# Mixer steps of an eight-head delta rule in another order: preparation in two parts, a denser solve, a later inverse, four heads' norms earlier

## What is computed

```python
# 8 heads of 128, 512 tokens in chunks; the reference uses chunks of 64, the kernel solves blocks of 128
q, k, v = silu(causal_depthwise_conv(qkv, conv_w, width=4)); q, k = l2_normalize(q), l2_normalize(k)
decay = exp(where(causal, gc_i - gc_j, -inf))           # gc: cumulated log decay per head
a_mat = where(strict, beta_i * (k k^T) * decay, 0)
u, w  = triangular_solve(a_mat + I, [beta v, beta exp(gc) k])
qk    = where(causal, (q k^T) * decay, 0)
for chunk: v_new = u - w S; o = q_dec S + qk v_new; S = S * exp(g_last) + k_dec^T v_new
o = rms_norm(o, dn_norm_g) * silu(z)
merged = sigmoid(g_pool) * (pool @ pool_proj) + sigmoid(g_dn) * (o @ dn_proj)
x = x + gate * (merged @ mix_w_out)
```

## Time and profile before

| | us |
|---|---|
| median of 3 runs | 1993.36 (1989.79 to 1993.92) |
| the profiled execution | 1994.52, span 1992.5 |
| TensorE busy | 1908.3 (96%) |
| VectorE busy | 915.5 (46%) |
| ScalarE busy | 810.4 (41%) |
| GpSimd busy | 130.6 (7%) |
| mean granted TensorE clock | 0.979 |

### The profile page before, as it was taken

One profiled execution on the slowest core, in us unless ns is written; L12 is line 12 of the kernel. 1 busy time (PEld: TensorE's weight loads), 2 busy tenths in 40 slices (PEclk: granted clock), 3 DMA queues, 4 the chain that ended last, 5 costly groups with the idle time before them and its releaser, 6 DMA issues.

```text
span 1992.5 us, 22201 instructions
## 1 busy us (share of the span) xinstructions
PE 1908.3 (96%) x8899; PEld 1467.7 (74%) x8899; DVE 915.5 (46%) x1644; ACT 810.4 (41%) x1324; POOL 130.6 (7%) x158
## 2 busy tenths in 40 slices
PE   7999999999989899999999998899899999999997
PEld 4666666666778788888876776777777878888886
DVE  4655566556433433333236765367244443333322
ACT  5555555556632322322224652463363333222221
POOL 0111111110001000000100010001000110000010
PEclk9999999999999999999999998999999999999999
DMA  5434333432232223222314222121212422322331
GB/s 207 159 129 151 136 143 131 150 127 94 85 128 95 76 95 104 95 95 91 102 41 164 85 75 64 38 74 59 64 43 95 140 82 96 96 95 95 95 98 61
DMA packets 56686, 201.95 MB, mean 101 GB/s; under 512 B 6639, under 2 KB 7095, under 8 KB 55945
## 3 DMA queue, kind: packets, MB, share of 16 engines
q1 hardware_dynamic: 44616, 158.32, 23.9%
q0 software_dynamic: 11968, 42.21, 5.9%
HBM read 195.23 MB, written 5.28 MB: 101 GB/s over the span
## 4 chain that ended last, share of the span: by engine, by line
PE 86%; DVE 6%; ACT 5%; DMA 2%; issue 1%; POOL 0%; SPq 0%; DVEq 0%; ACTq 0%; POOLq 0%
PE ps L1010 24%; PE ps L1013 24%; PE ps L1011 24%; PE ps L1061 2%; PE ps L1051 2%; PE ps L1097 2%; PE ps L1085 2%; DVE wL L1285 1%; DVE a L1556 1%; DVE a L1559 1%; PE ps L1073 1%; ACT wH L1630 1%; PE ps L1034 1%; PE ps L1140 1%; PE ps L1133 1%
## 5 line engine op out<-in xcount | busy, mean ns | idle before, releaser
L1010 PE MATMUL ps<-hH,wH 128*128 128x512 f32 (+1 forms) x1640 | 688.7, 420 | 20.0 <-DVE hL L1325 12.3
L1013 PE MATMUL ps<-hH,wL 128*128 128x512 f32 (+1 forms) x1640 | 647.5, 395 | 0.6 <-DVE wL L1285 0.6
L1011 PE MATMUL ps<-hL,wH 128*128 128x512 f32 (+1 forms) x1640 | 646.3, 394 | 0.0
L1285 DVE TENSOR_TENSOR wL<-wr,wH 128x1024 fp32r<-128x1024 f32 (+2 forms) x285 | 343.9, 1207 | 501.2 <-ACT wH L1630 501.1
L1630 ACT ACTIVATE wH<-wr 128x1024 fp32r<-128x1024 f32 (+2 forms) x285 | 295.2, 1036 | 279.7 <-PE ps L1013 267.5
L1010 PEld LDWEIGHTS ps<-hH,wH 128*128 128x128 f32 (+1 forms) x1640 | 312.5, 191 | 128.6 <-issue 61.5
L1011 PEld LDWEIGHTS ps<-hL,wH 128*128 128x128 f32 (+1 forms) x1640 | 312.3, 190 | 73.5 <-issue 14.9
L1013 PEld LDWEIGHTS ps<-hH,wL 128*128 128x128 f32 (+1 forms) x1640 | 311.1, 190 | 70.2 <-DVE wL L1285 2.0
L1013 PE MATMUL ps<-gffn,wL 128*128 128x512 f32 x352 | 137.0, 389 | 0.0
L1010 PE MATMUL ps<-gffn,wH 128*128 128x512 f32 x352 | 137.0, 389 | 0.0
L1011 PE MATMUL ps<-gffn,wH 128*128 128x512 f32 x352 | 136.9, 389 | 0.0
(11 more groups left out here) (286 smaller groups left out, 1958.6 us busy)
## 6 DMA issues: line engine op xcount, KB each, us to landing
wr<-wst SPq DMA_DIRECT2D x268, 512.0 KB, 3.5
a<-wfd POOLq DMA_DIRECT2D x54, 512.0 KB, 4.6
xT<-wfd POOLq DMA_DIRECT2D x18, 512.0 KB, 6.9
wr<-wst SPq DMA_DIRECT2D x16, 384.0 KB, 3.0
xT<-xin SPq DMA_DIRECT2D x8, 256.0 KB, 5.2
xT<-xin SPq DMA_DIRECT2D x2, 1024.0 KB, 6.0
xsave<-xT SPq DMA_DIRECT2D x1, 2048.0 KB, 8.9
a<-wfd POOLq DMA_DIRECT2D x8, 256.0 KB, 3.6
```

What stands on the lines that cost most here:

```text
L1010: e.matmul(o, hi, xh[k], start=k == 0, stop=False)
L1011: e.matmul(o, hi, xl[k], start=False, stop=False)
L1013: i = e.matmul(o, lo, xh[k], start=False, stop=k == t.nk - 1)
L1285: e.tensor_tensor(dst, x, hi.bitcast(F32), ALU.subtract).then_inc(s[name], 1)
```

## The change

- `out0`: `mod` comes after the fourth result tile, not inside the first.
- `conv_act` is due 6 ticks after the eighth k is begun, not 8.
- The sums of q come at Q+39+j (were Q+43+2j) and the norms of q at Q+44 (was Q+50).
- `prep` comes at Q+52+3j, a tick earlier, and only TensorE's three groups, VectorE's mask addition and ScalarE's exponentials stay in it. VectorE's three products and GpSimd's are a new step `prep_end` at Q+56+3j. ScalarE takes the four exponentials of `dt` before the one of the bank. `sol_send` goes to Q+66.
- The 30 `solve` steps take 20 ticks, not 30; `sol_back` is at Q+100 (was Q+110).
- The inverse begins at Q+125 (was Q+120), the recursion at Q+139 (was Q+134); in it one fill tick is added ahead of each `rec_r`.
- In the second half the squares and norms of heads 0 to 3 are put at Q+104 and Q+112, with other buffers (`hb`), and P5 and P6 wait for them. After the recursion heads 4 to 7 follow, the norms 8 ticks later; `zd_out` of heads 0 to 2 comes 2, 4 and 6 ticks after it, that of head 3 after 8, those of 4 to 7 as before.

```diff
             r = sig("xr")
             self.whole(Tile("res0", src("l0_w_out", 128 * c, 16), self.pb01.take()[1], "g", ("xr", r), c=c, xr=r),
-                       then=(lambda: square(c - 1)) if c > 0 else (lambda: add("mod")))
+                       then=(lambda: square(c - 1)) if c > 0 else None)
+            if c == 3:
+                add("mod")
...
                 if k == 7:
-                    at(clock[0] + 8, conv_act, a)
+                    at(clock[0] + 6, conv_act, a)
...
+        def prep_end(h):
+            add("prep_end", **heads[h]["prep"])
...
+        def head_squares(g):
+            add("head_squares", g=g, hq=[sig("hq") for _ in range(4)], oe=4 * g + 4)
...
                 at(at_k + 2 * j, l2_sum, h, kl)
-                at(Q + 43 + 2 * j, l2_sum, h, ql)
-                at(Q + 53 + 3 * j, prep, h)
+                at(Q + 39 + j, l2_sum, h, ql)
+                at(Q + 52 + 3 * j, prep, h)
+                at(Q + 56 + 3 * j, prep_end, h)
                 at(Q + 51 + 8 * j, v_turn, h)
             at(at_k + 7, l2, "k", kl)
-            at(Q + 50, l2, "q", ql)
-            at(Q + 63, lambda: add("sol_send", half=half, pa2=self.count["pa2"]))
+            at(Q + 44, l2, "q", ql)
+            at(Q + 66, lambda: add("sol_send", half=half, pa2=self.count["pa2"]))
             for k in range(1, 31):
-                at(Q + 79 + k, lambda k=k: add("solve", half=half, k=k))
-            at(Q + 110, lambda: add("sol_back", half=half))
+                at(Q + 79 + (2 * k) // 3, lambda k=k: add("solve", half=half, k=k))
+            at(Q + 100, lambda: add("sol_back", half=half))
             for j, step in enumerate(("t", "p5", "y5", "p6", "y6")):
-                at(Q + 120 + 3 * j, inverse, half, step)
+                at(Q + 125 + 3 * j, inverse, half, step)
+            if half == 1:
+                at(Q + 104, head_squares, 0)
+                at(Q + 112, head_norms, 0)
...
-            while clock[0] < Q + 134:
+            while clock[0] < Q + 139:
                 fill(1)
...
                 if t > 0:
+                    fill(1)
                     d["ks"], d["rr"] = sig("ks"), [sig("rr") for _ in range(4)]
...
-        add("head_squares", hq=[sig("hq") for _ in range(DNH)], oe=self.count["oe"])
...
+        head_squares(1)
         B = clock[0]
-        at(B + 6, head_norms, 0)
-        at(B + 13, head_norms, 1)
+        at(B + 8, head_norms, 1)
         for h in range(DNH):
-            at(B + 16 + 3 * h, zd_out, h)
+            at(B + 2 + 2 * h if h < 4 else B + 8 + 3 * h, zd_out, h)
...
+        hb = [P5[:, 0:512], P6[:, 0:512], P6[:, 512:1024], vT[0], tq[4], tq[5], tq[6], tq[7]]
...
                     e.tensor_tensor(v3(dt), v3(ps[b][:]), per4(C("mneg")), ALU.add).then_inc(s["px2"], 1)
+                elif what == "prep_end":
+                    hh = d["h"] % 4
+                    b, b2, b3 = d["banks"]
+                    at, dt = AT[hh], DT[d["dt"]]
                     w.wait_ge(s["pkk"], d["pkk"])
                     w.wait_ge(s["pxs"], d["pxs"])
...
                     w.wait_ge(s["px2"], d["px2"])
-                    e.activation(b[:], b[:], ACT.Exp).then_inc(s["px1"], 1)
                     w.wait_ge(s["bd"], 6)
                     for t in range(4):
                         col = 8 * t + d["h"]
                         i = e.activation(b4(dt, t), b4(dt, t), ACT.Exp, bias=ngc[:, col:col + 1])
                     i.then_inc(s["pxs"], 1)
+                    e.activation(b[:], b[:], ACT.Exp).then_inc(s["px1"], 1)
...
+                    w.wait_ge(s["oe"], d["oe"])
+                    if d["g"] == 0:
+                        w.wait_ge(s["dvt"], DNH)
+                    for h in range(4 * d["g"], 4 * d["g"] + 4):
+                        e.activation(hb[h], oD[h], ACT.Square).then_inc(s["hq"], 1)
...
-                elif what == "prep":
+                elif what == "prep_end":
                     at = AT[d["h"] % 4]
                     w.wait_ge(s["pa1"], d["pa1"])
```

More of the change, by code:

```diff
@@ L603, in inverse, with head_norms @@
             add("inv_" + step, half=half, **d)
+        def head_squares(g):
+            add("head_squares", g=g, hq=[sig("hq") for _ in range(4)], oe=4 * g + 4)
+        def head_norms(g):
+            items = [dict(h=h, bank=wk.take()[1], hq=h + 1, hm=sig("hm"), hl=sig("hl"), hx=sig("hx"), hn=sig("hn"))
+                     for h in range(4 * g, 4 * g + 4)]
+            add("head_norms", items=items)
         for half in range(2):
@@ L683, in mixer @@
         add("mix_out", om=self.count["om"], pp=8, m1=8)
-        add("head_squares", hq=[sig("hq") for _ in range(DNH)], oe=self.count["oe"])
-        def head_norms(g):
-            items = [dict(h=h, bank=wk.take()[1], hq=h + 1, hm=sig("hm"), hl=sig("hl"), hx=sig("hx"), hn=sig("hn"))
-                     for h in range(4 * g, 4 * g + 4)]
-            add("head_norms", items=items)
         def zd_out(h):
             add("zd_out", h=h, zdm=sig("zdm"), oh=sig("oh"), ol=sig("ol"))
+        head_squares(1)
         B = clock[0]
-        at(B + 6, head_norms, 0)
-        at(B + 13, head_norms, 1)
+        at(B + 8, head_norms, 1)
         for h in range(DNH):
-            at(B + 16 + 3 * h, zd_out, h)
+            at(B + 2 + 2 * h if h < 4 else B + 8 + 3 * h, zd_out, h)
         fill(10 ** 6)
@@ L1269, in _ @@
                         w.wait_ge(s["hq"], d["hq"])
-                        e.matmul(b[:], C("one128"), tq[d["h"]], start=True, stop=True).then_inc(s["hm"], 1)
+                        e.matmul(b[:], C("one128"), hb[d["h"]], start=True, stop=True).then_inc(s["hm"], 1)
         @block.vector
@@ L1531, in _ @@
                 elif what == "prep":
-                    hh = d["h"] % 4
-                    b, b2, b3 = d["banks"]
-                    at, dt = AT[hh], DT[d["dt"]]
+                    b, dt = d["banks"][0], DT[d["dt"]]
                     w.wait_ge(s["pr1"], d["pr1"])
@@ L1565, in _ @@
                     w.wait_ge(s["i5"], d["i5"])
+                    if d["half"] == 1:
+                        w.wait_ge(s["hn"], 4)
                     e.tensor_copy(P5[:], ps[d["banks"][0]][:]).then_inc(s["i5c"], 1)
@@ L1605, in _ @@
                         w.wait_ge(s["hx"], a["hx"])
-                        e.scalar_tensor_tensor(oD[h], oD[h], S("dn_g"), tr[h], ALU.mult, ALU.mult).then_inc(s["hn"], 1)
+                        e.scalar_tensor_tensor(oD[h], oD[h], S("dn_g"), hb[h], ALU.mult, ALU.mult).then_inc(s["hn"], 1)
                 elif what == "zd_out":
@@ L1870, in _ @@
                 elif what == "head_squares":
+                    w.wait_ge(s["oe"], d["oe"])
[3 more added lines that the diff above has]
+                        e.activation(hb[h], oD[h], ACT.Square).then_inc(s["hq"], 1)
+                elif what == "head_norms":
                     e.preload_act_table_set("natural_log_exp_and_others")
-                    w.wait_ge(s["oe"], d["oe"])
-                    for h in range(DNH):
-                        e.activation(tq[h], oD[h], ACT.Square).then_inc(s["hq"], 1)
-                elif what == "head_norms":
                     for a in d["items"]:
                         w.wait_ge(s["hm"], a["hm"])
-                        e.activation(tr[a["h"]], ps[a["bank"]][:], ACT.Ln, bias=C("eps")).then_inc(s["hl"], 1)
+                        e.activation(hb[a["h"]], ps[a["bank"]][:], ACT.Ln, bias=C("eps")).then_inc(s["hl"], 1)
                     for a in d["items"]:
                         w.wait_ge(s["hl"], a["hl"])
-                        e.activation(tr[a["h"]], tr[a["h"]], ACT.Exp, scale=-0.5).then_inc(s["hx"], 1)
+                        e.activation(hb[a["h"]], hb[a["h"]], ACT.Exp, scale=-0.5).then_inc(s["hx"], 1)
                 elif what == "out_zd":
```

## The result

| | before | after |
|---|---|---|
| median of 4 runs each | 1993.64 (1989.79 to 1994.79) | 1982.98 (1979.93 to 1983.49) |
| the profiled execution | 1994.52, span 1992.5 | 1979.93, span 1977.7 |
| mean granted TensorE clock | 0.979 | 0.983 |

The ratio is 0.9947, 95% interval 0.993 to 0.9964: 10.7 us less, where 9.4 were forecast. The profiled execution of the changed kernel was the fastest of its four, so the two profiles lie 14.8 us apart, not 10.7. In another set of runs, on another chip, the changed kernel took 1981.13 us beside 1993.56 before.

The account below looks back on a forecast made before the run. TensorE is busy 1908.3 of 1992.5 us, so other engines matter only where it stands still. Terms -7.3 + 2.7 + 4.3 - 3.3 - 5.9 = -9.5 us gave 1984 against the median; 8 in 10: 1965 to 1994.

Parts of the forecast that it names:

- Modulation row: Transpose of the modulation row, four tiles later: its 5.11 us DMA wait and the clock dip go, -7.3 us.
- Preparation: Mixer preparation in two parts: third preparation waits 7.1 us, fourth 1.1 us, and the solve starts 9.6 us later.
- Solve: Denser solve, first half: 24.2 us long, pool bank waits of 3.2 and 3.5 us replace the DMA wait, +2.7 us.
- Second half: Same places in the mixer's second half: solve 9.6 us later, inverse at 1417.4 against 1413.1 before, +4.3 us.
- Norms: Mixer's tail: four heads' norms move to the second half's solve, 2.5 us of waits left, -5.9 us.
- Inverse and recursion: First half: waits for VectorE and dips fall from 9.3 to 6.0 us, -3.3 us; second half 0.
- Rival 1: Split of the preparation works: TensorE finds its banks, the solve starts no later; -32 us in all, 1962; chance 0.14.
- Rival 4: A ScalarE table switch costs more than its load, four more switches on the way: +5.1 us, 1989; chance 0.05.
- Past a delay of some 2 us every us of delay costs one us in each half: Claim in the slower rival (20 us solve delay, +20.8, 2005, chance 0.08): pool products' banks hang on the solve's delay.

Follow-up runs that it names:

- The run with 2 ticks: Changed kernel with each head's second preparation part (`prep_end`) 2 ticks behind its first part, not 4: 1965.27 us, ratio 0.9856 to the kernel before.

## Why the prediction was right

The forecast was 1984, faster; the chip gave 1982.98. The sum was -9.5 where the two profiles differ by 14.8 and the medians by 10.7. The queue positions held; that the total came so near is in part luck. I compare term by term in the profiles, and use the medians for the whole.

- **Modulation row: right.** -7.3 predicted, 6.7 ahead at the first norm sum, -7.7 alone. Of the 6.7, 0.6 were lost by the start of the mixer.
- **Preparation: right to a few tenths in the first half.** The bank was forecast free at 1162.7 on the clock of before; it came at 1156.84, and with the 6.06 us that the kernel is ahead there that is 1162.9. Waits 7.1 and 1.1 predicted, 6.70 and 1.09 measured; last deferred part at 1181.0, measured 1175.10 + 6.06 = 1181.2; from it to the solve 12.05, measured 12.01; solve start 9.6 later, measured 9.75.
- **Solve: right.** 24.2 us long, measured 24.05. Waits at the pool banks 3.2 and 3.5 us, measured 3.15 and 3.08. Inverse at +2.7, measured 1229.15 - 6.06 = 1223.1 against 1225.94: +2.85.
- **Second half: the term of +4.3 was too high, it was +0.7 in this profile and +2.9 in the second one.** I carried the 9.6 us over from the first half; the third preparation waits 6.26 us there and the solve starts at 1369.69, which with 5.97 is 1375.7, 7.8 us later than in the earlier trace rows. That is 1.8 of the 3.6. The rest is the dip of 1.7 us that I had put behind the wait for the second pool product. Here that wait was 1.8 us and the clock was 1.00 from 1400 us to the inverse; in the second profile it was 3.1 us, with 0.90 from 1395 us to the inverse, and that is the 1.7. So the dip came in one execution of the two.
- **Norms: mis-sized, -5.9 predicted, -8.6 between the two second-half marks.** I left 2.5 us of waits in the tail; 1.0 was left, and no dip. (In the second profile it is 8.6 too.) The four sums take 0.9 us each, not the 0.45 I used; since I counted them on both sides this did no harm, but it hid a gain. While TensorE waits for the solve they are free: the run with the norms alone shows that wait 3.15 us shorter.
- **Inverse and recursion: right**, -3.3 predicted, 2.75 measured; P5's copy waits 2.52 us (2.65 predicted).

The two errors go the same way and make 6.3 us (3.6 and 2.7); the difference between the sum and the profiles is 5.3, since the other terms, the modulation row's above all, gave 1 less in all. Against the second profile, whose span is 12.8 us shorter than before, 3.3 us are missing, the norms' 2.7 above all. Against the medians little of it is seen, as the median of the changed kernel lies 3 us above its profiled execution. So the median flatters the sum, and that only 1 us lies between forecast and result is luck: by the profiles the sum fell short by 3.3 to 5.3 us.

**Rival 1, that the split works, was priced at 1962** (by the forecast's own step from the profile to the median it would be 1961) on the condition that TensorE finds its banks and the solve starts no later. The run with 2 ticks meets that condition in the main: the solve starts at 1174.33, the kernel before's at 1183.42, or 1175.9 when taken back by the 7.5 us by which this run's first `l2_sum` is ahead; the 3.3 us before v1's turn are left. It took 1965.3. The mechanism of the forecast was right and the price of the rival was near; only the ticks of `prep_end` decide between them. **Rival 4** is gone: between 1146.09 and 1150.6 of the changed kernel two loads lie between operations with hundredths of a us to either side:

```profile
1146.11 1.28 ACT L1817 ACT_TABLE_LOAD   x1
1147.40 0.63 ACT L1817 ACTIVATE a<-a 128x512 f32<-128x512 f32 x1
1148.05 1.28 ACT L1847 ACT_TABLE_LOAD   x1
1149.35 1.28 ACT L1847 ACTIVATE a<-a,tiny 128x128 f32<-128x128 f32 x4
```

A switch and back costs 2.6 us here and nothing beside the loads. The Trainium skill (ScalarE: Activation LUTs, What ACT_TABLE_LOAD costs) adds 1.38 us of drain to each; the gaps in these rows are 0.02 us or less, so the measurement decides against it for this chain.

**"Past a delay of some 2 us every us of delay costs one us in each half"** was too strict. With the 1.5 us ahead of the edit taken off, 11.3 us less delay moved the inverse by 8.0 us in the first half, and the whole kernel gained 15.9, that is 8 a half: as the preparation's waits go, one at the pool banks grows (4.4 us in each half, where 3.1 stood).

**What stays open.** The parts don't add: -21.2 alone, -10.7 and -12.4 together. The lists of waits show where some of it is. The norms alone take 3.15 us from the waits for the DMA, and with the solve denser and the inverse later there is nothing left to take. The preparation's delay is in part swallowed by these waits when it is alone (3.3 us), not in the whole kernel. That is 6.4 of about 10 us. The modulation row's run has 2.0 us less of them too, but that is within what they differ by between executions. And the tail works the other way (the denser solve alone loses 2.2 us there, which the moved norms avoid), so some 4 to 6 us have no name; each of the ratios is uncertain by 2 to 4 us, and I didn't measure pairs of parts.

## What to carry to other kernels

An in-order engine frees another engine's banks only when it gets to the operation in its queue. So ask of a deferred operation what stands ahead of it and what that waits for: here two ticks in the place of four small groups of products, against two convolutions and the mask additions of a half, cost 15.9 us, on an engine that is idle for half of the time. The Trainium skill (Perfetto Trace Analysis, Matmuls) advises to rotate matmul groups through banks so that one's evacuation overlaps the next; these groups rotate, and the trace agrees with it for the first two preparations, which don't wait; the third waits 6.70 us all the same, for a bank whose product stands behind a convolution on VectorE.

A wait that several parts of a change all shorten can be won only once. Before summing the terms, list for each which wait it shortens; a delay ahead of a wait is in part swallowed by it. And before a term of 2 us is judged from two profiles, look at a second profile of the same kernel: here one of its marks moved by 2.2 us.

Where two waits trade against each other (a product queued behind steps, the end of these steps), sweep the pace. With the second part right behind the first, 25, 27 and 30 ticks had the bank's wait fall from 3.1 us to 1.7 and to nothing and the DMA's come back (none, none, 4.2 and 2.3 us), with the best at 27, not at either end; 20 ticks were run only with the second part 2 and 4 ticks behind.

## What the runs showed of the hardware

- The length of a wait is not its price. With 3.1 us at the pool banks the granted clock over the two stretches was 0.95 and 0.98, with 1.7 us it was 0.98 and 1.00; the time fell by 6.4 us for 2.8 us of waits. Nor is the price fixed: the wait for the second half's first pool product was 4.18 us and the group behind it took 6.73 us in one execution of the changed kernel, 3.96 and 5.40 us in the other.
- The same round trip through DRAM (one write of 256 KB, four reads of 64 KB, first half) took 10.6 us from the write's issue to the inverse's first product in the kernel before and 9.3 us in the run with the norms alone, whose order is the same up to there.
- The write of the solve's results (256 KB to DRAM) kept GpSimd waiting for 2.64 us behind its issue with 27 ticks and 3.36 with 30, at the same size. With 30 ticks a weight load (512 KB) had been issued by SP at 1204.01, 1.1 us ahead of the write; with 27 it came at 1204.19, 0.9 us behind it. Whether that is the cause wasn't tried.
